# The weights that mix a head's three groups made once per token, and group 2's cached values on VectorE

## What is computed

```python
def _softmax_lse(logits):
    m = jnp.max(logits, axis=-1, keepdims=True)
    p = jnp.exp(logits - m)
    s = jnp.sum(p, axis=-1, keepdims=True)
    return p / s, (m + jnp.log(s))[..., 0]

def _combine_groups(outs, lses):
    w = jax.nn.softmax(jnp.stack(lses, 0), axis=0)
    return jnp.sum(w[..., None] * jnp.stack(outs, 0), axis=0)
```

## Time and profile before

| | |
|---|---|
| runs shown | 2101.2, 2101.74, 2103.39 us; median 2101.74 |
| profiled execution | 2106.31 us, of which the span is 2104.5 |
| granted TensorE clock | 0.992 of full speed |
| PE / DVE / ACT / POOL busy | 97% / 56% / 43% / 37% of the span |
| attention part | about 80 to 765 us of the span |
| DMA | 239.90 MB, mean 114 GB/s |

### The profile page before, as it was taken

How to read it: one execution, slowest core, us unless ns; L and a number is a source line. 1 busy time by engine, 2 the same in 40 slices (tenths; PEclk the granted TensorE clock), 3 DMA queues, 4 the chain that set the end, 5 groups by cost and what they waited for, 6 DMA issues and landing times.

```text
span 2104.5 us, 35573 instructions
## 1 busy us (share of the span) xinstructions
PE 2051.0 (97%) x14196; PEld 2017.6 (96%) x14196; DVE 1176.2 (56%) x1794; ACT 906.9 (43%) x1596; POOL 776.6 (37%) x594
## 2 busy tenths in 40 slices
PE   8999999999999999999999999999999899999998
PEld 6999999999999999999999999999999799999998
DVE  7433564565564542677722434767676667777643
ACT  6444354444453232666711234534344544444431
POOL 0111111111111122222232124555554699999821
PEclk9999999999999999999999999999999999999999
DMA  8124324324324212111111133243444655444232
GB/s 288 55 87 159 104 83 174 110 88 179 100 89 179 94 34 74 36 46 47 41 51 40 61 120 115 102 154 131 151 149 164 213 167 162 148 146 146 70 117 82
DMA packets 87511, 239.90 MB, mean 114 GB/s; under 512 B 11163, under 2 KB 23687, under 8 KB 85779
## 3 DMA queue, kind: packets, MB, share of 16 engines
q1 hardware_dynamic: 87348, 237.64, 33.8%
HBM read 185.21 MB, written 54.76 MB: 114 GB/s over the span
## 4 chain that ended last, share of the span: by engine, by line
PE 78%; POOL 9%; DMA 4%; DVE 4%; issue 3%; ACT 2%; SPq 0%; POOLq 0%; ACTq 0%; DVEq 0%
PE ps L1735 26%; PE ps L1150 23%; PE ps L1789 18%; POOL dn_lo L2182 4%; DMA dn_raw<-w_ds 3%; PE ps L1204 2%; PE ps L1188 2%; PE ps L1229 1%; POOL dn_raw L2194 1%; POOL dn_sum L2193 1%; PE ps L1250 1%; POOL dn_sum L2191 1%; PE ps L1220 1%; PE ps L1161 1%; POOL ssq L2177 1%
## 5 line engine op out<-in xcount | busy, mean ns | idle before, releaser
L1150 PE MATMUL ps<-act_lo,w_hi 128*128 128x352 f32 x1056 | 352.3, 334 | 1.5 <-ACT pe_stage L311 1.5
L1150 PE MATMUL ps<-act_hi,w_lo 128*128 128x352 f32 x1056 | 341.7, 324 | 0.0
L1150 PE MATMUL ps<-act_hi,w_hi 128*128 128x352 f32 x1056 | 340.9, 323 | 0.0
L736 POOL TENSOR_TENSOR w_lo<-w_raw,w_hi 128x1024 fp32r<-128x1024 f32 (+1 forms) x44 | 106.1, 2410 | 621.4 <-ACT w_hi L748 621.4
L2164 POOL TENSOR_TENSOR w_lo<-w_raw,w_hi 128x1024 fp32r<-128x1024 f32 (+1 forms) x54 | 133.3, 2469 | 385.8 <-ACT w_hi L1853 385.8
L1150 PEld LDWEIGHTS ps<-act_lo,w_hi 128*128 128x128 f32 x1056 | 200.1, 189 | 2.1 <-ACT pe_stage L311 1.8
L1150 PEld LDWEIGHTS ps<-act_hi,w_hi 128*128 128x128 f32 x1056 | 200.8, 190 | 0.0
L1789 PE MATMUL ps<-op_lo,dn_hi 128*128 128x264 f32 x896 | 185.0, 288 | 15.8 <-POOL dn_lo L2182 12.3
L1150 PEld LDWEIGHTS ps<-act_hi,w_lo 128*128 128x128 f32 x1056 | 199.8, 189 | 0.0
L1789 PE MATMUL ps<-op_lo,up_hi 128*128 128x264 f32 x896 | 183.5, 286 | 4.7 <-issue 3.0
L2335 DVE TENSOR_TENSOR x_res<-x_res,ps 128x528 f32<-128x528 f32 x208 | 141.5, 699 | 75.4 <-PE ps L1789 74.1
(11 more groups left out here) (324 smaller groups left out, 4464.1 us busy)
## 6 DMA issues: line engine op xcount, KB each, us to landing
hid_raw<-hid_dram SPq DMA_DIRECT2D x56, 528.0 KB, 4.2
w_raw<-w_qkv SPq DMA_DIRECT2D x36, 512.0 KB, 4.8
hid_dram<-hid_stage SPq DMA_DIRECT2D x16, 1056.0 KB, 5.0
up_raw<-w_us SPq DMA_DIRECT2D x32, 512.0 KB, 6.5
dn_raw<-w_ds SPq DMA_DIRECT2D x64, 256.0 KB, 3.3
hid_dram<-hid_stage SPq DMA_DIRECT2D x16, 792.0 KB, 3.5
kcache<-kc SPq DMA_DIRECT2D x16, 512.0 KB, 3.9
vcache<-vc SPq DMA_DIRECT2D x4, 2048.0 KB, 9.0
```

The lines of the kernel that those rows point to most:

```text
L736: pool.tensor_tensor(w_lo[:, b % 2, 0:nk], w_raw[:, b % 2, 0:nk], w_hi[:, b % 2, 0:nk].bitcast(F32), ALU.subtract).then_inc(S["wlo"], 1)
L1150: ins = pe.matmul(pj[c][:, 0:CH], w[:, b % 2, k], x[:, k, c * CH:(c + 1) * CH], start=k == 0 and x is act_lo, stop=k == KD - 1 and w is w_lo)
```

## The change

- `load_weights` becomes four steps. `store_lse` (SP, slot 1 of the group 0 step) stores `lse_row`; `load_mix` (SP, slot 3) reads the 3 x 1056 values back with a *token* per partition, 8 tokens and the sample's in 9 columns (`mix`, 128 x 27), by four DMAs whose patterns undo the group order: runs of 8 values for group 0, single values for groups 1 and 2; on `mix` DVE does maximum and difference (`less_max`, slot 5), ACT the exponential (`weights`, slot 6), DVE sum, reciprocal and product (`divide`, slot 7), seven operations of 9 or 27 columns on DVE in all; `store_mix` (SP, slot 8) writes the finished weights to `mix_dram` in group order by four DMAs of the same patterns, and `load_weights` (SP, now slot 0 of the group 1 step) broadcasts them into `e_bc`.
- `max_lse`, the wide `less_max`, `denominators`, `invert` and the last product of `combine` go.
- Group 2's cached values are taken as group 1's: no transpose L1217 and no L1250 for it; its cache lies in DRAM with the head dimension first; `store_probs` also in slot 8 of group 2 steps, `load_probs` also in slot 0 of the next group 0 step, `cached_values` also in slots 4 to 7 of that step.

```diff
-                if g == 1:
-                    wait(sp, "vals_done", j)
+                if g:
+                    wait(sp, "vals_done", max(turn(s) - 1, 0))
...
+        def by_token(dram, g, width):
+
+            n = NP_ // STRIDE[g]
+            at = dram.offset + g * width
+            dims = {1: [[8, P], [1, 8]], 4: [[2, P], [1, 2], [n, 4]], 8: [[1, P], [n, 8]]}[STRIDE[g]]
+            return bass.AP(dram.tensor, at, dims)
...
+        def load_mix(jj):
+
+            sp.wait_ge(S["lse_stored"], 16 * (jj + 1))
+            wait(sp, "mix_stored", 16 * (NG + 1) * jj)
...
+            for g in range(NG):
+                sp.dma_start(mix_part(g), by_token(lse_dram, g, SLOTS * P), allow_slow_non_contiguous=True).then_inc(S["mix_loaded"], 16)
+            sp.dma_start(mix[0:NS, :, SLOTS - 1], samples(lse_dram, SLOTS * P), allow_slow_non_contiguous=True).then_inc(S["mix_loaded"], 16)
+
+        def store_mix(jj):
+
+            sp.wait_ge(S["mixed"], jj + 1)
+            wait(sp, "e_loaded", 16 * NG * jj)
+            for g in range(NG):
+                sp.dma_start(by_token(mix_dram, g, T), mix_part(g), allow_slow_non_contiguous=True).then_inc(S["mix_stored"], 16)
+            sp.dma_start(samples(mix_dram, T), mix[0:NS, :, SLOTS - 1], allow_slow_non_contiguous=True).then_inc(S["mix_stored"], 16)
+
         def load_weights(jj):
 
-            sp.wait_ge(S["lse_copied"], jj + 1)
-            sp.wait_ge(*since("vals_done", jj + 1))
-            sp.dma_start(lse_dram, lse_row[:]).then_inc(S["lse_stored"], 16)
-            sp.wait_ge(S["lse_stored"], 16 * (jj + 1))
+            sp.wait_ge(S["mix_stored"], 16 * (NG + 1) * (jj + 1))
+            sp.wait_ge(*since("vals_done", 2 * (jj + 1)))
             for g in range(NG):
-                sp.dma_start(e[:, g], bass.AP(lse_dram.tensor, lse_dram.offset + g * SLOTS * P, [[0, P], [1, T]])).then_inc(S["e_loaded"], 16)
+                sp.dma_start(e[:, g], bass.AP(mix_dram.tensor, mix_dram.offset + g * T, [[0, P], [1, T]])).then_inc(S["e_loaded"], 16)
...
-                if cur < NSTEP and g == 2 and i == 0:
+                if 0 < cur <= NSTEP and g != 1 and i == 0:
                     load_probs(cur - 1)
-                if cur < NSTEP and g == 1 and i == SLOTS - 1:
+                if cur < NSTEP and g and i == SLOTS - 1:
                     store_probs(cur)
...
-                if i == 1 and g == 0 and j:
+                if g == 0 and j:
+                    if i == 1:
+                        store_lse(j - 1)
+                    elif i == 3:
+                        load_mix(j - 1)
+                    elif i == 8:
+                        store_mix(j - 1)
+                if i == 0 and g == 1 and j:
                     load_weights(j - 1)
...
-                if core and cur % NG == 2 and 4 <= i < 8:
+                if 0 < cur <= NSTEP and cur % NG != 1 and 4 <= i < 8:
                     cached_values(cur - 1, i - 4)
...
-                if g == 1:
+                if g:
                     pe.matmul(pO[:, 0:NS], v[0:NS, TL], pt[0:NS, 1, 0:NS], start=True, stop=True).then_inc(S["o_psum"], 1)
                     return
...
-            if g == 1:
+            if g:
                 return
```

More of the change, by code:

```diff
@@ L149, in build @@
         probs_dram = nc.dram_tensor("probs_dram", (NS, P), F32, kind="Internal").ap()
+        mix_dram = nc.dram_tensor("mix_dram", (NG * T,), F32, kind="Internal").ap()
         lse_dram = nc.dram_tensor("lse_dram", (NG * SLOTS, P), F32, kind="Internal").ap()
@@ L468, in attention @@
     bias_dram, lse_dram, att_dram = shared["bias_dram"], shared["lse_dram"], shared["att_dram"]
-    probs_dram = shared["probs_dram"]
+    probs_dram, mix_dram = shared["probs_dram"], shared["mix_dram"]
     NSTEP = HG * NG
@@ L692, in load_probs @@
+            wait(sp, "comb", s // NG)
+            wait(sp, "vals_done", turn(s))
             sp.dma_start(probs[:].rearrange("p s k -> p (s k)"),
@@ L807, in weights @@
         def weights(jj):
[L808 to L816, removed]
+            act.wait_ge(S["sub"], jj + 1)
+            act.activation(mix[:], mix[:], ACT.Exp).then_inc(S["ex"], 1)
         def body(cur, nxt, i):
@@ L846, in body @@
                     log_sums(j - 1)
-                if g == 0 and j and i == 8:
+                if g == 0 and j and i == 6:
                     weights(j - 1)
-                if g == 1 and j and i == 2:
-                    invert(j - 1)
         def copy_gate(s, i):
@@ L932, in copy_values @@
             dve.wait_ge(S["vt_psum"], 3 * s + t + 1)
-            if s and (s - 1) % NG == 1:
+            if s and (s - 1) % NG:
                 wait(dve, "o_psum", PAIRS * s)
@@ L936, in copy_values @@
                 wait(dve, "o_psum", PAIRS * s - 1)
-                wait(dve, "new_used", s - (s + 1) // NG)
+                wait(dve, "new_used", (s + 2) // NG)
             if t < 2:
@@ L970, in maxima @@
             wait(dve, "pt_psum", PAIRS * s if p == 0 else n - 1)
-            if p == 0 and g == 2:
-                wait(dve, "probs_stored", 16 * (s // NG + 1))
+            if p == 0 and s and g != 1:
+                wait(dve, "probs_stored", 16 * (turn(s - 1) + 1))
             wait(dve, "exp_done", n)
@@ L1045, in denominators, with one, less_max @@
+        def one():
+            return mix_one[:].unsqueeze(1).to_broadcast([P, NG, SLOTS])
+        def less_max(jj):
+            dve.wait_ge(S["mix_loaded"], 16 * (NG + 1) * (jj + 1))
+            over_groups(ALU.max, jj, "mix_max")
+            dve.tensor_tensor(mix[:], mix[:], one(), ALU.subtract).then_inc(S["sub"], 1)
+        def divide(jj):
             dve.wait_ge(S["ex"], jj + 1)
-            over_groups(ALU.add, jj, g, ("den_a", "den")[g - 1])
+            over_groups(ALU.add, jj, "mix_sum")
+            dve.reciprocal(mix_one[:], mix_one[:]).then_inc(S["rec"], 1)
+            dve.wait_ge(S["rec"], jj + 1)
+            dve.tensor_tensor(mix[:], mix[:], one(), ALU.mult).then_inc(S["mixed"], 1)
@@ L1048, in weigh @@
         def weigh(jj, g):
-            dve.wait_ge(S["ex"], jj + 1)
-            if g == 1:
-                dve.wait_ge(*since("vals_done", jj + 1))
+            dve.wait_ge(S["e_loaded"], 16 * NG * (jj + 1))
+            if g:
+                dve.wait_ge(*since("vals_done", 2 * jj + g))
             dst = o_of(jj, g)
@@ L1057, in combine @@
                 dve.wait_ge(S["prod"], 3 * (jj + 1))
-                dve.wait_ge(S["rec"], jj + 1)
-            g, done = ((1, "comb_a"), (2, "comb_b"))[part]
+            else:
+                dve.wait_ge(S["comb_a"], jj + 1)
+            g, done = ((1, "comb_a"), (2, "comb"))[part]
             dst, og = o0[jj % 2], o_of(jj, g)
@@ L1062, in combine @@
             dve.tensor_tensor(dst[:, NP_:T], dst[:, NP_:T], og[:, NP_:T], ALU.add).then_inc(S[done], 1)
-            dve.wait_ge(S[done], jj + 1)
-            if part == 1:
-                dve.tensor_tensor(dst[:], dst[:], mx[:], ALU.mult).then_inc(S["comb"], 1)
         def split_head(j):
@@ L1102, in body @@
                 if g == 0 and j:
-                    if i in (3, 4):
-                        max_lse(j - 1, i - 2)
-                    elif i in (5, 6, 7):
-                        less_max(j - 1, i - 5)
+                    if i == 5:
+                        less_max(j - 1)
+                    elif i == 7:
+                        divide(j - 1)
                 if g == 1 and j:
-                    if i < 2:
-                        denominators(j - 1, i + 1)
-                    elif i == 2:
+                    if i == 2:
                         weigh(j - 1, 0)
@@ L2584, in layout @@
         out[f"kc{g}"] = c[:, :, 0].transpose(2, 3, 0, 1)
-        out[f"vc{g}"] = c[:, :, 1].transpose((2, 3, 0, 1) if g == 1 else (2, 1, 0, 3))
+        out[f"vc{g}"] = c[:, :, 1].transpose((2, 3, 0, 1) if g else (2, 1, 0, 3))
     xb, yb, ga, gb = (tiles(w_in[:, att + D * n:att + D * (n + 1)]) for n in range(4))
```

77 lines of the change are left out of this document (38 added, 39 removed).

## The result

The changed kernel takes **2142.96 us** (median of 4 runs, 2142.31 to 2145.55) beside 2101.49 for the kernel before in the same session: 1.0194 times as long, 95% interval 1.0181 to 1.0207, slower by 41 us where the forecast was 13 us faster. The profiled execution took 2145.55 us. First the page of the changed kernel: its span, busy times, the row of PE's granted clock, the count of packets and the chain that ended last, to be held against the earlier trace rows.

The account below looks back on a forecast made before the run. PE, busy 97% of the span, was taken to bound the kernel as a single chain of its own instructions. Terms -13.8 + 0.9 = -12.9 us gave a median of 2088.8 us from 2101.74, range 2086.0 to 2096.0.

Parts of the forecast that it names:

- the landing of `store_mix`: Four small stores of finished weights from SP: estimated to land in 3.2 us after issue, adding no wait.
- 72 ns a run: Upper estimate for the weight store, 2.3 / 32 with nothing fixed: 10.2 us to land.
- Second rival: Slow element-wise store makes `load_weights` delay the cached keys in slot 0; up to 18.3 us, 2107.1 us; chance 0.07.
- The 6.3 us until SP comes to the broadcast: Time from finished weights at 291.1 to SP reaching `load_weights` at 297.4; a store's excess is paid in three steps.
- That is cover with nothing to spare; I charge zero: Cached keys behind 1.6 MB of broadcast in group 1 steps: landing by 305.5, PE wanting them at 305.34; charged zero.
- Rival 4: A later stage or more frequent half-clock stretches of PE absorb the gain; at its fullest about 2101.7 us; chance 0.06.
- PE's removed work: Group 2's small matmuls (13.4 us) and transpose L1217 (0.44 us) leave PE in four heads: 13.8 us saved.
- the signs of being right: Listed trace signs: 64 fewer small products, PE attention waits below 6 us, store landing within 4 us, attention ending 13 us earlier.
- DVE's cover in the group 0 steps: DVE's idle time hides its added work in slots 5 and 7 of group 0 steps; 0.9 us charged in all.
- rival 1: DVE late in group 0's slots 5 and 7, making PE wait; up to 10.2 us in place of 0.9; chance 0.14.
- L1258's wait: PE's wait for L1018, the `lse` addition queued on DVE behind `copy_values`: 2.6 us, three times, said to stay.
- The end has 6.3 us of slack: Last head: mixed head ready at 758.9, ACT taking it only at 765.19, 6.3 us later; no cost charged.

Follow-up runs that it names:

- e4: The changed kernel with each of the 2048 single values of groups 1 and 2 stored 512 B apart in another tensor, log-sum-exps broadcast instead of weights; 2114.18 us.
- e3: The changed kernel with the broadcast of the weights issued behind the cached keys of slots 0 and 1; 2136.15 us, ratio 1.0162.
- e1: The changed kernel with weights stored in token order, 480 runs in place of 2272, and DVE reading the broadcast tile with a stride; 2105.55 us.
- e11: The kernel before, with only slot 0's cached keys in the four group 1 steps requested late, when PE needs them; 2129.74 us beside 2101.38.
- e5: e1 with the broadcast of the weights issued behind the cached keys of slots 0 and 1; 2096.29 us beside 2103.03.
- e7: e5 with group 2's cached values back on PE; 2103.16 us, ratio 0.9997.
- e2: e1 with group 2's cached values back on PE; 2110.66 us, ratio 1.0041.
- e8: e5 with the small log-sum-exp addition moved on DVE ahead of the copy of v in slot 1; 2092.95 us, ratio 0.9945.
- e9: e8 with the group 1 step's weighing and adding spread over slots 2 to 5 in place of 2 to 4; 2088.67 us beside 2101.38.

## Why the prediction was wrong

1. **The step that failed is the landing of `store_mix`.** The forecast took 3.2 us, a slope of 8 ns a run from the earlier trace rows, and 10.2 us as the bound from above. It was 17.2 us (15.7 to 17.2 over the four heads), beyond both. The slope came from runs of 128 and 512 B, 8 and 32 for each engine; nothing in the trace wrote single values. The bound "72 ns a run" was no bound, since it too was made of 512 B runs. The Trainium skill ("DMA: Bandwidth & Descriptors", rules for kernel authors, and specifications) warned of this pattern, an element per descriptor and read-modify-write under 512 B. The trace agrees in part: the profile's packets under 512 B rose from 11163 to 29979 (nearly half of the rise are the reads), and e4's 5.9 to 9.6 us against 15.7 to 17.2 fits writes into shared stretches as the dearer ones; but reads of the same pattern cost 3.6 us, which the rule doesn't tell apart. That a read-modify-write is what costs, no run here shows.
2. **Second rival, right in place and sign, too small in price.** It named the wait in slot 0 ahead of the cached keys and gave 2107.1, at 0.07. Missing was what e3 shows, that the transfers behind the store are slow in themselves. The 6.3 us until SP comes to the broadcast were right (e1: 287.90 to 294.22), but PE began to pay before a store used them up, because of point 3.
3. **"That is cover with nothing to spare; I charge zero"** failed on its own. Even with a store of 5.5 us (e1) the keys landed 8.6 us after their issue, not the 6.8 assumed, and PE waited 9.0 us in three steps.
4. **A wait was priced at its length.** For waits of 3 to 4 us e11 gives nearly twice that. Rival 4 named half-clock stretches that fall more often and held them to be worth the whole gain at most; they came, but as what follows PE's waits.
5. **What held.** PE's removed work (13.8 us: 132 records fewer, where the signs of being right say 64 small products, a slip against the earlier trace rows's 128; e5 against e7 agrees within a few us); DVE's cover in the group 0 steps (no new wait of PE there in any version; rival 1 falls, but the 2.6 us in front of `divide` made the keys later, as e2 shows); the tiny operations (0.16 to 0.19 us); the second read of probabilities; L1258's wait, unchanged at 2.6 us, until e8 took it away. "The end has 6.3 us of slack" was right in kind, and used up.

Chances of 0.87 to 0.07 were too sure for a sum whose one unmeasured term sat on a path with no slack and no bound from above.

## What to carry to other kernels

Undo a permutation on the side that reads: single values read from DRAM were cheap here (a median of 3.6 us to land), single values written were not (16 to 17 us), and they held up whatever was queued behind. On a kernel that PE bounds, put the transfers that PE needs ahead of any that can wait, and price a new wait of PE of a few us at up to twice its length. When a term rests on an operation that the trace doesn't have, ask how much slack its path has before asking for its likely size: e9, which keeps the idea and mends the two places, is 0.6% faster than the kernel before.

## What the runs showed of the hardware that was not expected

- A store of 12 KB in single values lands 15.7 to 17.2 us after its last issue; in runs of 32 B 4.5 to 5.5 us (e1); with the values 512 B apart 5.9 to 9.6 us (e4).
- Behind such a store a weight block of 512 KB took 17.5 us to land in place of 4.7, and an ordinary load of 0.65 us issue time took up to 5.4 us to issue (e3), so the delay reaches SP itself.
- A wait of PE of 3.7 us is followed by about 10 us at half clock (e11), though the clock was full while PE stood; without the wait there were 3.4 us at half clock in the same step.
- Two scalings on DVE that start beside a 2.4 us subtraction on POOL take 2.6 us in place of 0.55.
